# Second cross-attention: order of GpSimd's key and value load, and VectorE's look-ahead over the query chunks

## What is computed

```
for i in range(DEPTH):                     # DEPTH = 2
    x = x + Mixer_i(rms_norm(x, norm_mix[i]))       # RG-LRU (0), Mamba-2 SSD (1)
    x = x + mem_attend(rms_norm(x, norm_mem[i]), mk, mv, mem_w_q[i], mem_w_o[i])
    x = x + FFN_i(rms_norm(x, norm_ffn[i]))         # SwiGLU (0), top-2-of-8 experts (1)

def rms_norm(x, g):
    y = xf * lax.rsqrt(jnp.mean(xf * xf, axis=-1, keepdims=True) + EPS)
    return y * g

def mem_attend(h, k, v, w_q, w_o):         # 4 heads of 256, 256 memory tokens
    q = (h @ w_q).reshape(B, T, MEM_HEADS, MEM_HD)
    s = jnp.einsum('bthd,bmhd->bhtm', q, k) * (MEM_HD ** -0.5)
    o = jnp.einsum('bhtm,bmhd->bthd', softmax(s), v)
    return o @ w_o
```

## Time and profile before

| | |
|---|---|
| median of 3 runs (lowest, highest) | 1989.22 us (1987.37, 1998.58) |
| the profiled execution: its time, its span | 1987.67 us, 1985.9 us |
| mean granted TensorE clock of it | 0.966 of full |
| attention of layer 0, `norm` to the last query result taken out | 209.43 to 234.50 us |
| the same in layer 1 | 844.78 to 873.31 us |

### The profile page before, as it was taken

How to read it: one execution, slowest core, us unless ns; L and a number is a source line. 1 busy time by engine, 2 the same in 40 slices (tenths; PEclk the granted TensorE clock), 3 DMA queues, 4 the chain that set the end, 5 groups by cost and what they waited for, 6 DMA issues and landing times.

```text
span 1985.9 us, 31992 instructions
## 1 busy us (share of the span) xinstructions
PE 1852.8 (93%) x10920; PEld 1596.0 (80%) x10920; DVE 1466.5 (74%) x1764; ACT 1244.4 (63%) x1603; POOL 186.1 (9%) x227
## 2 busy tenths in 40 slices
PE   6998989999899997998599999999999999999994
PEld 6997869999799776887388888888888888888883
DVE  7588446663588568433499898988988889898884
ACT  6575245443475254312487888878888787877873
POOL 3021111000134510101100000000000000000001
PEclk9999989999899998998799999999999999999997
DMA  7647588754443931556399999999999999999993
GB/s 264 233 130 244 216 326 339 269 166 149 160 135 130 340 109 44 197 212 238 115 401 371 385 356 377 372 360 391 360 375 372 362 389 364 385 358 371 379 371 142
DMA packets 151104, 558.73 MB, mean 281 GB/s; under 512 B 16496, under 2 KB 16496, under 8 KB 149568
## 3 DMA queue, kind: packets, MB, share of 16 engines
q1 hardware_dynamic: 139248, 508.58, 69.2%
q10 hardware_dynamic: 6832, 28.44, 3.5%
q0 software_dynamic: 4896, 20.18, 2.7%
HBM read 520.61 MB, written 36.52 MB: 281 GB/s over the span
## 4 chain that ended last, share of the span: by engine, by line
PE 80%; issue 7%; DVE 7%; DMA 3%; ACT 2%; POOL 1%; POOLq 0%; SPq 0%; ACTq 0%; DVEq 0%
PE ps L1728 24%; PE ps L1730 24%; PE ps L1729 24%; DVE w_lo L1106 2%; PE ps L2143 1%; PE ps L2028 1%; DMA raw<-in_stream 1%; PE ps L1827 1%; PE ps L1858 1%; POOL rt L2187 1%; PE ps L1874 1%; DMA y_rows<-ye 1%; PE ps L1759 1%; ACT w_hi L700 1%; PE ps L1849 0%
## 5 line engine op out<-in xcount | busy, mean ns | idle before, releaser
L1629 DVE TENSOR_TENSOR w_lo<-raw,w_hi 128x1024 fp32r<-128x1024 f32 x672 | 786.5, 1219 | 49.4 <-ACT w_hi L1036 47.7
L1036 ACT ACTIVATE w_hi<-raw 128x1024 fp32r<-128x1024 f32 x672 | 704.5, 1060 | 139.6 <-PE ps L1730 123.7
L1728 PE MATMUL ps<-w_hi,xe_hi 128*128 128x512 f32 x896 | 358.2, 400 | 4.7 <-DVE w_lo L1629 4.7
L1730 PE MATMUL ps<-w_hi,xe_lo 128*128 128x512 f32 x896 | 354.5, 396 | 0.0
L1729 PE MATMUL ps<-w_lo,xe_hi 128*128 128x512 f32 x896 | 354.0, 395 | 0.0
L700 ACT ACTIVATE w_hi<-raw 128x1024 fp32r<-128x1024 f32 x212 | 220.5, 1050 | 166.3 <-PE ps L1730 116.8
L1106 DVE TENSOR_TENSOR w_lo<-raw,w_hi 128x1024 fp32r<-128x1024 f32 x212 | 266.3, 1269 | 69.6 <-ACT w_hi L700 69.1
L1728 PE MATMUL ps<-h_hi,w_hi 128*128 128x288 f32 x928 | 280.0, 302 | 11.2 <-DVE w_lo L1106 6.8
L1729 PE MATMUL ps<-h_lo,w_hi 128*128 128x288 f32 x928 | 275.8, 297 | 0.0
L1730 PE MATMUL ps<-h_hi,w_lo 128*128 128x288 f32 x928 | 274.9, 296 | 0.0
L1728 PEld LDWEIGHTS ps<-w_hi,xe_hi 128*128 128x128 f32 x896 | 168.9, 189 | 43.1 <-DVE w_lo L1629 5.1
(11 more groups left out here) (396 smaller groups left out, 2550.8 us busy)
## 6 DMA issues: line engine op xcount, KB each, us to landing
raw<-in_experts SPq DMA_DIRECT2D x672, 512.0 KB, 5.5
raw<-in_stream SPq DMA_DIRECT2D x261, 512.0 KB, 4.5
rest<-in_stream SPq DMA_DIRECT2D x28, 512.0 KB, 10.6
x_rows<-zeros ACTq DMA_DIRECT2D x1, 13824.0 KB, 58.9
out_ssd_s<-s_new ACTq DMA_DIRECT2D x16, 512.0 KB, 7.0
xs<-x_rows POOLq DMA_DIRECT2D x9, 512.0 KB, 4.7
y_rows<-ye POOLq DMA_DIRECT2D x9, 512.0 KB, 7.4
out_k<-kmem ACTq DMA_DIRECT2D x2, 1024.0 KB, 7.4
```

Of the source, the lines that this page charges most:

```text
L1036: act.activation(w_hi[:, (NSPLIT + p) % HL, :], raw[:, slot, :], ACT.Copy) \
L1629: dve.tensor_tensor(w_lo[:, (NSPLIT + p) % HL, :], raw[:, (NRING + p) % RAW, :], w_hi[:, (NSPLIT + p) % HL, :].bitcast(F32), ALU.subtract) \
L1728: pe.matmul(out, l_hi, r_hi, start=start, stop=False)
L1730: return pe.matmul(out, l_lo, r_hi, start=False, stop=stop)
```

## The change

`behind` gets another value for the query results: `ORDER[NEED[g]] + HL - 2`, at most `AHEAD[g]`. GpSimd's additions leave `zero_attention` and are called beside it. In layer 0 they stay behind `load_kv(0)`; in layer 1 they stand ahead of the wait for the last `ssd out` and of `load_kv(1)`.

```diff
@@ -1108,6 +1108,8 @@
             def behind(g):
+                if PLAN[g][0][0] == "q":
+                    return min(AHEAD[g], ORDER[NEED[g]] + HL - 2)
                 return max(ORDER[NEED[g]], AHEAD[g] - 1)
@@ -2222,7 +2224,6 @@
             def zero_attention(l):
 
-                add_squares(3 * l + 1, h)
                 pool.wait_ge(full, KEY["norm", 3 * l + 1] + 1)
@@ -2233,6 +2234,7 @@
             load_kv(0)
+            add_squares(1, h)
             zero_attention(0)
@@ -2301,6 +2303,7 @@
                 pool.wait_ge(state_out[k], 16 * (NB // 2))
+            add_squares(4, h)
             pool.wait_ge(full, KEY["ssd out", KD - 1] + 1)
             load_kv(1)
             zero_attention(1)
```

## The result

The changed kernel takes 1983.15 us (median of 12 runs, 1970.51 to 1988.96); the kernel before, run beside it, 1996.57 us (median of 12, 1983.71 to 1999.97). The ratio is 0.9943 with an interval of 0.9921 to 0.9964. So the kernel is faster by about as much as I forecast (13.4 us between the medians, 13.0 forecast), but its time lies 8.5 us above the forecast of 1974.7 us and outside the range of 1971 to 1980.5.

The account below looks back on a forecast made before the run. TensorE, busy for 93% of the span, was taken to bound the kernel. Its idle time and clock gave 5.55 + 1.95 + 3.51 + 2.00 = 13.0 us: 1987.67 − 13.0 = 1974.7 us, range 1971 to 1980.5.

Parts of the forecast that it names:

- GpSimd's additions (5.55 us): Layer 1, ahead of `norm`: additions put before the loads take out TensorE's whole 5.55 us of idle time.
- The clock behind `norm` (1.95 us): Layer 1, `norm` to q6's taking out: without the idle time ahead, the full clock returns, gaining 1.95 us.
- q7 (3.51 and 2.00 us): q6 to q7: VectorE's earlier split gains 3.51 us in layer 1 (about 1.5 from the clock), 2.00 in layer 0.
- the clock does not come back: Rival: low-clock stretches stay or as much is lost elsewhere; 9.5 us gain left, 1978.2 us; chance 0.14.
- the sum: Both attentions: 5.55 + 1.95 + 3.51 + 2.00 = 13.0 us gained, giving 1974.7 us from the profiled 1987.67.
- The four terms together: Both attentions: idle time ahead of `norm`, clock behind it, and q7 in each layer gain 13.0 us; chance 0.68.
- What spoke against it: Layer 1, end of q0: additions beside VectorE's work could hold up `h_lo`, costing 1.0 us, 1975.7 us; chance 0.09.
- given back at the cache: Rival, tail of the values: TensorE waits longer there for all 13.0 us, 1987.7 us, no change; chance 0.03.

Follow-up runs that it names:

- the first execution: The unchanged kernel before, in the profiled execution from which the prediction started: 1987.67 us.
- the second: The kernel before, nothing changed, profiled again: 1988.15 us.
- the third: The kernel before, nothing changed, profiled once more: 1999.72 us.
- before's fourth execution: The kernel before, nothing changed, in the last of its three extra profiles: 2000.87 us.

## Why the prediction was right, and where it failed

**GpSimd's additions (5.55 us): right.** q0's start to `norm` takes 844.22 − 840.81 = 3.41 us, before 844.78 − 835.48 = 9.30: 5.89 us. The kernel with this part alone has it, the one without it has the 5.55 us wait.

**The clock behind `norm` (1.95 us) and q7 (3.51 and 2.00 us): right.** From `norm` to q7 out both layers take 23.07 us (layer 0: 206.99 to 230.06), before 25.07 and 28.53: 2.00 and 5.46 us. The rival "the clock does not come back" did not happen here. Two sizes depend on the execution. Of the 3.51 us, the 1.5 us for the low clock are not there to win in every run: in the kernel before VectorE had 5.12 us of idle time ahead of q7 in layer 1 of the first execution, in both layers of the second, and 3.61 us in both layers of the third and fourth. And the low clock behind `norm` cost more in the third: 878.03 − 855.40 = 22.63 us to q6's taking out, 2.76 more than the 19.87 of layer 0, not 1.95. From that execution the sum would have been 5.55 + 2.76 + 2.00 + 2.00 = 12.3 us.

**The four terms together: right.** 5.89 + 5.46 + 2.00 = 13.35 us against 13.0.

**What spoke against it: did not happen.** The last addition took 0.81 us, the short end of 0.81 to 1.68, and was done 0.87 us before `norm` began. `h_lo` beside it took 0.74 us and ended at 843.66 us; TensorE's load of weights waited 0.18 us for it, against 0.36 before. That `h_lo` began inside the addition (842.92 us, within 842.54 to 843.35) I took, in the prediction too, as speaking against the rule of the Trainium skill (page "SBUF — State Buffer", section "Who interferes with whom"). It settles less than that: most others took 0.51 us, so this one was 0.23 us longer, and if it had worked only after the recorded end of the addition it would have ended at 843.86 us, 0.20 later than it did. The profile gives GpSimd's spans only roughly, so that neither confirms nor refutes the rule; an addition of 1.68 us was not there to show its price of 1.0 us. The loads were issued at 843.30 and 843.86 us, landed after 5.7 and 8.6 us, and nothing waited for them. The tail of the values kept 4.3 us of waits (4.6 before), so next to nothing was given back at the cache: 6.0 us ahead before it, 5.7 behind it.

**The sum: failed.** The step that failed is "I forecast the median of the changed kernel at the sum". It took the profiled execution of 1987.67 us as the kernel's time, since the lowest run was 0.3 us from it, and 1998.58 us as a stray. That run belonged to the commoner group: the chunk at half clock, 11.5 us more, in 7 of the 12 runs of the kernel before by their times, and 9 of 12 after. The sum does hold for the changed kernel's executions with the chunk at full clock: 1974.21 us profiled, and by their times three runs from 1970.5 to 1974.0. From the median of all runs before, 1996.57 − 13.0 gives 1983.6 us, 0.4 us from what was measured; that it is so close is in part luck, since the two medians also hang on the shares of the groups.

**The clock rival was too small.** I gave 3.5 us to low stretches that stay or turn up elsewhere, priced from the two short ones in the attention of layer 1. One stretch in the chunk costs 28.1 − 16.6 = 11.5 us. The rows shown held none in the chunk, since the execution before had none there; the time of 1998.58 us was the only hint of it, and I had no second profile.

**What stays open.** What decides in one execution whether the chunk runs at half clock. The wait ahead of the first masked tile goes along with it, and a short low stretch just ahead (698.7 to 705.5 us in the kernel before) makes TensorE arrive later and wait less; but the edit for a longer wait did not always bring it, and before's fourth execution (701.7 to 705.1 us) and the one with that edit (701.4 to 704.8 us) had such a stretch and the half clock too.

## What to carry to other kernels

An engine that is hardly busy can still hold up the busiest one by the order of its queue: work that keeps step with a producer belongs ahead of loads that have time to spare (here the last landed at 852.5 us, and the scores needed it after 867.3), and a look-ahead that leaves out the last chunk shows as one wait per layer. Before a forecast in absolute time, see whether the few runs of the kernel before lie in one group; if they don't, forecast the difference and add it to the median of many runs, or read a profile of each group. Where a wait stands ahead of a stretch that runs at half clock in some executions, a few products without use ahead of it can be worth more than the wait itself: here eight of them took 9.2 us from the median of the kernel before (1995.98 to 1986.79), by taking out a loss of 11.5 us in the executions that had it.

## What was unexpected of the hardware

TensorE was recorded as busy for 27.54 of 28.1 us in the chunk and was granted half the clock nearly throughout (0.53). I had taken low stretches for a thing of idle time. Here the clock fell during a wait of 2.25 us, at 703.8 us, and stayed low for 27 us while TensorE worked. In all five profiled executions with the half clock in the chunk it rose during the four products for the state; in the kernel before at full clock, and in the changed kernel at half, these took

```profile
722.52 3.70 PE L2067 MATMUL ps<-xd,bt 128*128 128x512 f32 x8
727.12 5.68 PE L2069 MATMUL ps<-xd,bt 128*128 128x512 f32 x8
```

The eight filling products kept the clock full in all three profiled executions that had them (the one with ten fillings among them), in one with 1.26 us of idle time left. And the same program has executions 11 to 12 us apart mostly for this, 0.6% of its time and nearly as much as the whole change gains.
